# Sliding-window attention weights turned by VectorE blocks and on-chip DMAs, with their product with V one body later

## The reference

```python
s = jnp.einsum('bnqhgd,bnkhd->bnhgqk', qb, kw).astype(jnp.float32) * (D ** -0.5)
s = jnp.where(valid[None, :, None, None], s, NEG_INF)          # window of 128 keys, 256 candidates per block
m = jnp.maximum(jnp.max(s, axis=-1, keepdims=True), sink)
e = jnp.exp(s - m)
p = e / (jnp.sum(e, axis=-1, keepdims=True) + jnp.exp(sink - m))
o = jnp.einsum('bnhgqk,bnkhd->bnqhgd', p.astype(v.dtype), vw)
...
x = x + (y * jax.nn.silu(gate)) @ w_out                        # y is o, flattened
```

## Time and profile before

| | |
|---|---|
| profiled execution | 2123.53 us, span 2121.7 us |
| PE, DVE, ACT, POOL busy | 2111.6, 1424.4, 966.3, 192.2 us |
| TensorE's granted clock, mean | 0.999 |
| SWA bodies 1 to 16 | 771.8 to about 1198 us of the span |

### The profile page before, as it was taken

The page is one execution under the profiler, slowest core; times in us unless marked ns, Lnnn a source line. Parts: engine busy times, 40 slices in busy tenths (PEclk is TensorE's granted clock), DMA queues, the critical chain, the costliest instruction groups (busy, mean ns, idle before and its releaser), DMA issues. The chain is left out here.

```text
span 2121.7 us, 30686 instructions
## 1 busy us (share of the span) xinstructions
PE 2111.6 (100%) x9996; PEld 1765.3 (83%) x9996; DVE 1424.4 (67%) x2667; ACT 966.3 (46%) x1876; POOL 192.2 (9%) x197
## 2 busy tenths in 40 slices
PE   9999999999999999999999999999999999999999
PEld 7888888888888888888888888888888888888887
DVE  6677777777633578888888733777777676769432
ACT  6444444445323345555555533544544445446221
POOL 0101111113011010000000122200000000003000
PEclk9999999999999999999999999999999999999999
DMA  7334443346635423333333733532324233335742
GB/s 229 95 81 117 113 109 109 109 111 192 179 85 144 140 80 89 89 89 89 89 89 89 237 97 101 184 87 80 111 85 117 60 111 91 88 103 154 209 118 69
DMA packets 388402, 244.95 MB, mean 115 GB/s; under 512 B 13312, under 2 KB 361216, under 8 KB 388352
## 3 DMA queue, kind: packets, MB, share of 16 engines
q1 hardware_dynamic: 382592, 239.39, 39.5%
q10 hardware_dynamic: 5760, 4.92, 0.9%
HBM read 210.33 MB, written 24.12 MB: 110 GB/s over the span
## 5 line engine op out<-in xcount | busy, mean ns | idle before, releaser
L637 PE MATMUL pp<-act_hi,w_hi 128*128 128x512 f32 x2304 | 906.2, 393 | 3.6 <-DVE w_lo L611 2.1
L639 PE MATMUL pp<-act_hi,w_lo 128*128 128x512 f32 x2304 | 898.6, 390 | 0.0
L638 PE MATMUL pp<-act_lo,w_hi 128*128 128x512 f32 x2304 | 898.3, 390 | 0.0
L611 DVE TENSOR_TENSOR w_lo<-raw,w_hi 128x512 fp32r<-128x512 f32 x680 | 455.5, 703 | 299.4 <-ACT w_hi L603 298.3
L603 ACT ACTIVATE w_hi<-raw 128x512 fp32r<-128x512 f32 (+1 forms) x684 | 395.5, 624 | 420.7 <-PE pp L639 201.3
L637 PEld LDWEIGHTS pp<-act_hi,w_hi 128*128 128x128 f32 x2304 | 433.4, 188 | 92.7 <-DVE w_lo L611 2.8
L639 PEld LDWEIGHTS pp<-act_hi,w_lo 128*128 128x128 f32 x2304 | 432.9, 188 | 91.2
L638 PEld LDWEIGHTS pp<-act_lo,w_hi 128*128 128x128 f32 x2304 | 433.6, 188 | 85.4 <-issue 0.2
L1980 ACT ACTIVATE s_prob<-ps,s_minus 128x256 f32<-128x256 f32 x96 | 44.6, 470 | 105.0 <-DVE s_minus L2059 97.9
L656 POOL TENSOR_TENSOR pT_lo<-gathered,pT_hi 128x640 fp32r<-128x640 f32 x30 | 46.5, 1570 | 358.7 <-ACT pT_hi L652 358.7
L1302 ACT ACTIVATE prob<-ps,minus,q_scale 128x512 f32<-128x512 f32 (+1 forms) x64 | 39.0, 615 | 78.3 <-DVE minus L1382 78.3
(11 more groups left out here) (419 smaller groups left out, 2803.9 us busy)
## 6 DMA issues: line engine op xcount, KB each, us to landing
raw<-w_in SPq DMA_DIRECT2D x48, 1024.0 KB, 5.9
raw<-swa_w_in SPq DMA_DIRECT2D x36, 1024.0 KB, 5.6
raw<-mla_w_in SPq DMA_DIRECT2D x23, 1024.0 KB, 5.8
raw<-mla_w_out SPq DMA_DIRECT2D x16, 1024.0 KB, 6.6
raw<-swa_w_out SPq DMA_DIRECT2D x16, 1024.0 KB, 6.3
raw<-w_out SPq DMA_DIRECT2D x16, 1024.0 KB, 7.1
x_feature_major<-xT SPq DMA_DIRECT2D x8, 1024.0 KB, 9.6
y_whole<-y_feature_major SPq DMA_DIRECT2D x7, 1024.0 KB, 6.9
```

Of the source, the lines that this page charges most:

```text
L611: q.eng.tensor_tensor(dst, raw_piece(tile, p), high, ALU.subtract).then_inc(s_lo, tile.ups(p))
L637: q.eng.matmul(psum[:, :], wh, ah, start=start and n == 0, stop=False)
L638: q.eng.matmul(psum[:, :], wh, al, start=False, stop=False)
L639: last = q.eng.matmul(psum[:, :], wl, ah, start=False, stop=stop and n == PIECE // P - 1)
```

## The change

For pairs 0 to 14 the 14 transposes leave PE. ACT now normalises (`normalise` in `swa_A`, Identity with a scale, four of 128 x 256 per head), DVE turns the 32 x 32 blocks of both heads into `turned` (`turn_pair`: one transpose of 128 columns and one of 768 per head), and SP issues 16 DMAs of 32 x 448 elements (`gather`) in the same body. At the end of the body ACT copies the whole `gathered` (128 x 1792) to `s_pT_hi`; in the next body DVE subtracts (128 x 1792) for `s_pT_lo`, and PE does the product with V of the pair before (`pv_prev`) between pieces 2 and 3 of its query tile, into other PSUM banks. `y_prev` is stored one body later. Pair 15, in body 16, still goes by PE's transposes and `pv`, so that body now has two products with V. The factor 0.5 moves from the normalisation to the last multiplication. All scores stand at the start of a body. POOL prepares the keys one body ahead, and copies `pair` after `pv_prev`. `pipelined` now writes body 1 out by itself.

```diff
+    def turn_pair(q, h):
+        rows = turned[:, :].rearrange("p (g n) -> p g n", g=QUADS)
+        for block, slot, n in ((0, 0, 1), (2, 1, 6)):
+            at = (7 * h + slot) * Q32
+            out_ = rows[:, :, at:at + n * Q32].rearrange("p g (b n) -> p b g n", n=Q32)
+            in_ = s_prob[:, h, block * P:(block + n) * P].rearrange("p (b g n) -> p b g n", g=QUADS, n=Q32)
+            m = q.eng.transpose(out_, in_)
...
 # PE
             def turn(h):
-                if attn:
-                    q.eng.wait_ge(*q.at(f"V.norm{h}"))
+                if not proj:
+                    if h == 0:
+                        q.eng.wait_ge(*q.at("V.y_prev"))
+                    q.eng.wait_ge(*q.at(f"A.norm{h}"))
...
+            def pv_prev():
+                q.eng.wait_ge(*q.at("V.lo_prev"))
+                q.eng.wait_ge(*q.at("G.pair", i - 1))
...
             piece(q_tile, 2, pp[0])
+            if not proj:
+                q.eng.wait_ge(*q.at("V.gate"))
+                early_output(q, 2, 1, 2)
+            pv_prev()
             piece(q_tile, 3, pp[0])
             if not proj:
-                q.eng.wait_ge(*q.at("V.gate"))
-                early_output(q, 2, 1, 3)
+                early_output(q, 2, 2, 3)
...
 # ACT
+            def normalise(h):
+                q.eng.wait_ge(*q.at(f"V.inv{h}"))
+                for b in range(NB):
+                    pr = s_prob[:, h, b * 2 * P:(b + 1) * 2 * P]
+                    m = q.eng.activation(pr, pr, ACT.Identity, scale=s_inv[:, h, b:b + 1])
+            def gathered_hi():
+                    for half in range(2):
+                        q.eng.wait_ge(s_turned[half], ...)
+                    copy_hi(q, s_pT_hi[:, :], gathered[:, :], "turned_hi", rest=True)
...
             next_hi(2)
+            gathered_hi()
             next_hi(3)
...
 # SP
+                if k == 0:
                     gather(units - 1)
+            if phase == "swa":
+                store_y(q, phase, units - 1, units - 3)
             for part in range(3):
                 load_y(q, n, part)
...
 # POOL
+                if prev:
+                    q.eng.wait_ge(*q.at("T.pv_prev1"))
                 for place, src in ((0, s_v_hi), (1, s_v_lo)):
                     m = q.eng.tensor_copy(pair[:, :, place, :], ...)
```

More of the change, by code:

```diff
@@ L139 @@
     "swa": {
[L140 to L146, removed]
+        "T": "s00 s01 s10 s11 pv_prev0 pv_prev1 t00 t01 t10 t11 pv0 pv1".split(),
+        "A": ("exp00 exp01 exp02 exp03 sink0 exp10 exp11 exp12 exp13 sink1 norm0 norm1 tanh low_prev0 low_prev1 pt_hi00 "
+              "pt_hi01 pt_hi10 pt_hi11 q_hi0 q_hi1 turned_hi y_low0 y_low1").split(),
+        "V": ("gate ready0 minus00 minus01 ready1 minus10 minus11 sum0 inv0 sum1 inv1 lo_prev turned sum_prev00 sum_prev01 "
+              "sum_prev10 sum_prev11 y_prev silu pt_lo00 pt_lo01 pt_lo10 pt_lo11 q_cos q_turn q_sin qr q_lo0 q_lo1 "
+              "y_sum00 y_sum01 y_sum10 y_sum11 y").split(),
+        "G": "sink keys pair".split(),
     },
@@ L1472, in pipelined @@
                 body(q, 0, True, False)
-                with loop(q.eng, 1, units) as i:
+                body(q, 1, True, True)
+                with loop(q.eng, 2, units) as i:
                     body(q, i, True, True)
@@ L1909, in turn @@
                     m.then_inc(*q.did(f"t{h}1"))
+            def pv_prev():
+                if not attn or (isinstance(i, int) and i == 1):
+                    return
+                q.eng.wait_ge(*q.at("V.lo_prev"))
+                q.eng.wait_ge(*q.at("G.pair", i - 1))
+                for half, parts in enumerate((((0, 0, 0, 2), (1, 2, 1, 1)), ((2, 4, 0, 2), (1, 3, 0, 1), (3, 6, 1, 1)))):
+                    bank = PAIR_BANK[half]
+                    for n, (j, at, to, blocks) in enumerate(parts):
+                        both = pair[:, j, :, :].rearrange("p d n -> p (d n)")
+                        q.eng.matmul(pair_tokens(bank[:, :], to, blocks), both, pair_slots(s_pT_hi, at, blocks),
+                                     start=n == 0, stop=False, skip_group_check=True)
+                        m = q.eng.matmul(pair_tokens(bank[0:HD2, :], to, blocks), pair[:, j, 0, :], pair_slots(s_pT_lo, at, blocks),
+                                         start=False, stop=n == len(parts) - 1, skip_group_check=True)
+                    m.then_inc(*q.did(f"pv_prev{half}", rest=half == 1 and proj))
             def pv():
-                if attn:
+                if not proj:
                     q.eng.wait_ge(*q.at("V.pt_lo11"))
@@ L1932, in swa_T @@
             scores(1, 0)
+            scores(1, 1)
             if attn:
@@ L2051, in maxima @@
                 if attn:
[L2052 to L2056, removed]
+                    if half == 0:
+                        q.eng.wait_ge(*q.at(f"T.s{h}1"))
+                        if h == 0:
+                            q.eng.wait_ge(*q.at("G.sink", i))
+                        q.eng.wait_ge(*q.at(("V.gate", "V.minus01")[h]))
+                        q.eng.sem_inc(*q.did(f"ready{h}"))
                     for b in (2 * half, 2 * half + 1):
@@ L2089, in swa_V, with sum_prev @@
                 q.eng.tensor_tensor(s_gate, pp[1][:, :], rstd[:, :], ALU.mult).then_inc(*q.did("gate"))
+            def sum_prev(half):
+                q.eng.wait_ge(*q.at(f"A.low_prev{half}"))
+                for h in range(2):
+                    to = s_y_sum[h * HD2:(h + 1) * HD2, half * 2 * P:(half + 1) * 2 * P]
+                    q.eng.tensor_tensor(to.rearrange("p (b a n) -> p b a n", b=2, a=QUADS), head_tokens(PAIR_BANK[half][0:HD2, :], h),
+                                        head_tokens(s_y_low[0:HD2, half, :], h), ALU.add).then_inc(*q.did(f"sum_prev{half}{h}"))
+            prev = attn and (not isinstance(i, int) or i >= 2)
             maxima(0, 0)
```

154 lines of the change are left out of this document (93 added, 61 removed).

## The result

The changed kernel took 2131.93 us (median of 8 runs, 2130.67 to 2132.95) against 2124.22 us for the kernel before (8 runs, 2123.45 to 2126.16) on the same chip: ratio 1.0035, 95% interval 1.0024 to 1.0045. It is 7.7 us slower, where 4.2 us faster was forecast. I compare from that score on. The kernel before was run again beside the variants, with medians of 2124.11 to 2124.52 us, so times of different variants can be compared to some 0.4 us.

What follows compares the result with a forecast made beforehand. PE was taken as the bound in every SWA body. The loop's -23.0 us and the end's +5.9 + 7.0 + 4.7 + 1.6 - 0.4 summed to -4.2, giving 2120.5 us, range 2113 to 2131.

Steps and rivals of the forecast that it cites:

- term 2: In the loop, the exchange between bodies stays hidden behind PE's work, SP issuing at 0.46 us each: price 0.
- the ring: In the loop, the chain turned, gather, ACT's copy, last splits, gate, maxima, turned, from one body to the next.
- rival R1: In the loop, that chain becomes the period, from an SP pace of 0.6: 2134 us, pace alone 2128.7; chance 0.18.
- Term (a): In body 16, y loads wait for gather and y store, so PE starts the output tiles later: 5.9 us.
- Term 1: In the loop, PE loses 14 transposes of 1.53 us in bodies 1 to 15: 23.0 us gained, period 25.37.
- Term (b): In body 16, PE waits for `lo_prev`, which comes after ACT's splits and exponentials and DVE's subtraction: 7.0 us.
- A: The time when the first y load has landed for body 16, forecast at T15 + 31.8 = T16 + 6.4.
- Term (c): In body 16, POOL's four `y_lo` chunks stand behind its copy of `pair`, which waits for `pv_prev`: 4.7 us.
- Term (d): In body 16, PE's clock falls after idle waits, slowing some 7 us of matmuls: 1.6 us.
- The sum of the end: In body 16, the costs 5.9 + 7.0 + 4.7 + 1.6 - 0.4, some 19 of the 23 us given back.
- R3: At the layer's end, no wait at all, needing issues that cost nearly nothing: 2101.7 us; chance 0.05.

Runs made afterwards that it cites:

- the three forms: Changed kernel with 8 of its 16 gather DMAs whole, 4 with a quarter of each row, 4 with a quarter of the rows: 2133.66 us.

## Why the prediction was wrong

T15 and T16 are the first scores of bodies 15 and 16, as in the prediction.

**The step that failed is the pace of SP in term 2, 0.46 us per issue.** SP took 0.63 with nobody beside it. I had read the 0.62 of the earlier trace rows as two queues hindering each other and took the pace of another kind of DMA; the three forms, and the two queues at 0.62 and 0.64, show that it is the price of one such DMA on its own queue. Two things follow from that one number.
- The loop: the ring of rival R1, 11.8 + 15p + 1.9 + 2.75, gives 25.84 us with p = 0.626, which is the period measured. That it fits to 0.01 is partly luck: its parts measured 11.5 (gate to first issue, 980.89 to 992.35), 9.4, 2.1 and 2.9, and their errors cancel. Against 25.37 the period is 0.47 us too long in 13 bodies and 1.3 in body 2, 7.4 us together. With 12 DMAs taken away, or with all 16 on two queues, it is 25.4. R1's mechanism was right, with its 0.18 too small a chance.
- Term (a) measured 10.3 us (1172.34 is T16 + 12.2, before T16 + 1.9) where 5.9 stood: the gather took 10.3 us, not 7.4, and began at T15 + 13.1, not T15 + 12.0, pushed by the ring (with four DMAs it began 12.1 us after the first score). The store (6.8 against 6.2) and the load (5.7) were near their prices.

**Right.** Term 1: body 1, which has no ring behind it, took 23.70 us, that is 26.90 less 1.53 and the 1.61 that moved, 23.76. Term (b): `pv_prev` began 13.9 us after ACT's first split of y, where A + 13.8 stood; from the first output matmul to it are 12.4 us, less two pieces of 2.72, 7.0, as forecast. Only 3.8 of these show as a wait, and not 7, since the two pieces ran slowly in the rest.

**Term (c), 4.7,** was right in its mechanism and nearly in its size: with PE kept warm the stretch behind `pv_prev` took 7.8 us for 2.9 us of matmuls, 4.9 too long, all of it at POOL's chunks. In the changed kernel it was 5.8. Of the 0.9 more, some 0.5 are POOL's chunks, 6.32 us for four and not 5.87, and 0.4 the last three matmuls at the low clock.

**Term (d), 1.6,** came out near what was on the path (2 us at the mark, 2.6 in the medians when PE was kept warm), but by luck. It took the start's mean clock of 0.78, where body 16 had 0.50 and 0.68, and so priced the slow matmuls far below the some 7 us that they cost; and it did not see that most of these would run ahead of waits which would have been there anyway.

The sum of the end was 18.8 and is 23.0. (a) alone is 4.4 over and (c) 1.1; (d), of which 1.0 is in `pv_prev` and the rest inside (b) and (c), is 0.6 under. Another 0.6 us are not assigned.

**Together:** the forecast of -4.2, with 7.4 more for the loop and 4.2 more for the end, makes +7.4; measured +7.7. The range was meant to reach R1 with the pace alone, but R1 was priced too low: by its own ring, 13 times 0.53 in the loop and 2.7 for the gather are 9.6, which is 2130.1 and not 2128.7, and the later start of the gather comes on top. The time is 0.9 us above the range.

Two smaller slips decided nothing: the first maximum of the earlier trace rows stands at T + 1.1, not 1.2, and the eight normalisations of 0.38 fill T + 7.3 to T + 10.4 with no room for the two splits between them.

R3's page rule, the Trainium skill's "DMA: Bandwidth & Descriptors", section "Issuing engines are not separate DMA queues", is that the sequencer's time to start a DMA is usually small beside the DMA. It was not so for these 16 small DMAs in a row: 10.02 us to issue, 2.0 us from issue to landing. Splitting them over two issuing engines took 5 us off the exchange.

## What to carry to other kernels

Count the issues: the 16 small DMAs here cost 16 times one issue, with whole blocks or quarters, and the price of one is best taken from the same kind of DMA in the trace, even where another queue was busy beside it. When a consumer is moved one iteration later, follow the last iteration on its own: what was hidden there (stores, loads, another engine's chunks behind a new wait) has nothing to hide behind; letting pair 14 go the old way, with the store at its right place, took 18 us off the changed kernel here. Matmuls that ran slowly ahead of a wait for another engine were free here, so price a low clock only where nothing else is late. DMA issues on a computing engine cost what stands behind them in its order, so put them ahead of an idle stretch: 8 issues at one place made the changed kernel 3.9 us slower, at another its variant 6.0 faster.

## What the runs showed of the hardware

- An issue of a DMA from SBUF to SBUF (32 rows of 1792 bytes) costs SP or ACT 0.62 to 0.64 us, with a quarter of the bytes in each row 0.62, with a quarter of the rows 0.68, and SP's pace stays 0.62 beside a second issuing queue; a weight load of 1 MB costs 0.38.
- VectorE's instructions that read two operands in SBUF took 1.65 to 1.76 us in place of 0.68 or 0.69 beside POOL's subtraction, which itself took 6.32 us for four (5.04 with the chunks first, 5.77). Maxima that read PSUM kept their spacing of 0.47 us beside POOL, in the kernel with the chunks first. The Trainium skill, "GPSIMD Engine Reference", section "8. Key points", says that the two share SBUF interfaces, with contention for VectorE instructions with two SBUF inputs; the trace agrees.
- Of some 7 us that matmuls lost in body 16 at a granted clock of 0.50 to 0.68, keeping the clock at 1.00 gave back 2 to 2.6: the slow ones ahead of the wait for `lo_prev` had cost nothing.
